# Second block of a two-block transformer kernel: plain float32 matmuls in place of three split products, a weight ring of eight slots, convolution taps and attention heads laid further ahead

## The chip, the cores and the metric

The kernel runs on one core of one Trainium2 chip. The metric is the device time of one launch in microseconds (us). The core has TensorE (PE in the profile, with PEld for its weight loads), VectorE (DVE), ScalarE (ACT), GpSimd (POOL), SyncE (SP, which only starts transfers here) and 16 DMA engines.

## The reference, cut to what matters

Two blocks run one after the other on 256 tokens of width 1024, in float32. The first (latent attention, Fourier and pooling branches, then a mixture over 16,384 experts whose rows are gathered) is not touched by the change. The second is this, with `T` = 256, `D` = 1024 and `D_FF` = 2816:

```python
for layer in range(2):
    f = swiglu_ffn(rms_norm(x, pre[layer, 0]), w_gate_up[layer, 0], w_down[layer, 0])
    x = x + 0.5 * rms_norm(f, post[layer, 0])
    h = rms_norm(x, mix_norm_pre[layer])
    if layer < 1:      # w_in 1024 -> 2048, GLU, causal convolution of 31 taps, LayerNorm, silu, w_out
        y = conformer_conv(h, ...)
    else:              # 8 heads of 128; with 256 tokens there is one block of keys, the own one
        q = h @ w_q;  k, v = split(rms_norm(x, g_kv) @ w_kv)
        y = causal_alibi_attention(q, k, v) @ w_o
    x = x + rms_norm(y, mix_norm_post[layer])
    f = swiglu_ffn(rms_norm(x, pre[layer, 1]), w_gate_up[layer, 1], w_down[layer, 1])
    x = x + 0.5 * rms_norm(f, post[layer, 1])
```

`swiglu_ffn(h)` is `(silu(gate) * up) @ w_down` with `gate, up = split(h @ w_gate_up)`.

## The kernel before, in words

Each engine has a program of its own, written out in one order of stages (`ORDER` for the first block, `ORDER2` for the second). The second block's stages are, for each of the six parts `f0`, `cv`, `f1`, `f2`, `at`, `f3`: `pre` (the norm, on DVE and ACT), `hT2` (16 transposes on PE), the part's inner stages, and `post` (norm and residual). Inner stages are `gu` and `dn` for a feed-forward part, `cin`, `taps`, `ln`, `cout` for the convolution, `qkv`, `moba`, `ao` for the attention.

Weights come in chunks of 1 MB (128 partitions x 2048 float32), 160 in all: 22 for each `gu`, 11 for each `dn`, 8 for `cin`, 12 for `qkv`, 4 for `cout` and 4 for `ao`. SP loads them into a ring of four slots (`SLOTS2`), three in `wring` and one in `rows`. In `gu`, `cin` and the k and q thirds of `qkv` (104 chunks) a chunk is used by `two_tiles`: 16 products, each with 128x128 weights stationary and 256 tokens moving. In `dn`, `cout`, `ao` and the v third of `qkv` (56 chunks) a chunk is used in 8 products, with the activations stationary and 512 weight columns moving.

Each product is made of three (`product`, lines 866 to 868). Both operands are split into an upper part of type float32r and a lower one (value minus upper part), and PE adds upper x upper, lower x upper and upper x lower. ACT writes the upper part of a chunk (`upper_of`, line 1288), DVE then the lower part (`lower_of`, line 1718); the transposed activations are split likewise (ACT line 1297, DVE line 1731), and so are the hidden values of a feed-forward part (DVE lines 1749 and 1751), the normed convolution output (1873, 1874) and each head's output (1396, 1895). `AHEAD` = 2 is how many chunks are split ahead of their use. The `gu` stages are hardware loops of five turns with four chunks each.

The products of the first block that are not gathers (for instance `gpre`, line 753, with the same shapes as `two_tiles`), the taps on PE (line 971) and the heads' scores and weighted sums (lines 1020 and 1036) are plain float32 matmuls.

In `cin` DVE and ACT make the gated values of 8 channel tiles; in `taps` DVE convolves four of them (31 steps each, line 1842) while PE convolves the other four by 124 matmuls with diagonal matrices, which ACT writes (line 1350) into a ring `diag` of 16. In `moba`, for head `hh`, PE makes the scores (1020), DVE adds the bias and takes the maximum (`biased`: 1887, 1890), ACT the exponential (1389), DVE reciprocal and scaling (1904, 1906), PE the transposes (1031) and the weighted sum (1036). Scores and `biased` run one head ahead.

SP's queue is in order. Ahead of the first chunk of the second block stand two loads of norm gains that wait for the first block's last residual (`x2` at 2).

## Time and profile before

| | |
|---|---|
| device time, median of 3 runs | 4663.01 us (4657.65 to 4663.29) |
| span of the profiled execution, first to last instruction | 4655.2 us |
| of it the second block (from 3461 us on) | 1194.2 us |
| PE busy over the span | 3150.5 us |
| PE busy in the second block | 1035.77 us |
| DVE and ACT busy in the second block | 694.50 and 464.94 us |

Of the profiled execution the span is what is known; it lies 7.8 us under the median of the three timed runs, and 2.5 us under the fastest. Changes are worked out on the span and carried over to the median. A busy PE is not a PE at its peak: a matmul's record holds its latency too, so consecutive records overlap, and what a product costs in a stream is read from the distance between starts.

### The profile page before, as it was taken

The page shows a single profiled execution, that of the slowest core. Times are in us where ns is not written, and L with a number is a line of the kernel's source. Part 1 is how long each engine was busy: PE and PEld are TensorE (multiplying, and loading weights), DVE is VectorE, ACT ScalarE, POOL GpSimd, SP SyncE. Part 2 cuts the span into 40 slices and gives each one's busy share as a digit, 9 for nine tenths or more (in the row PEclk, how much of TensorE's full clock was granted, in tenths as well). Part 3 has the DMA queues.
Part 4 walks back from the last instruction along what each step waited for, and adds up shares of the span by engine and source line. Part 5 has one row for each costly group of instructions (what it writes and reads, how often), then busy time and mean ns, then how long its engine had stood idle before and what let it go on. Part 6 is the DMA issues. An engine that isn't in the chain of part 4 may idle for free.

```text
span 4655.2 us, 42615 instructions
## 1 busy us (share of the span) xinstructions
PE 3150.5 (68%) x12636; PEld 1972.1 (42%) x12636; DVE 2902.3 (62%) x5798; ACT 961.8 (21%) x1932; POOL 1806.1 (39%) x1732
## 2 busy tenths in 40 slices
PE   6998346588755455555878633434449878898789
PEld 2476112254431111222535511111119768797688
DVE  2213996656689676666644788776666566565365
ACT  1211012111111001111122111111123353333333
POOL 0000566656566555666630277777740000000000
PEclk8999668799877777777889866677669989999799
DMA  4343779889988888889962588899975514544244
GB/s 187 137 151 134 234 264 343 299 339 358 333 321 298 313 322 333 306 322 345 382 246 87 172 305 304 315 337 343 345 289 173 176 42 158 188 166 172 82 167 154
DMA packets 273567, 1157.10 MB, mean 249 GB/s; under 512 B 30848, under 2 KB 31616, under 8 KB 234496
## 3 DMA queue, kind: packets, MB, share of 16 engines
q0 software_dynamic: 221184, 805.40, 47.9%
q1 hardware_dynamic: 52224, 349.75, 20.9%
q8 instruction: 78, 1.28, 0.1%
q14 instruction: 81, 0.66, 0.0%
HBM read 1153.99 MB, written 1.05 MB: 248 GB/s over the span
## 4 chain that ended last, share of the span: by engine, by line
PE 40%; DVE 24%; DMA 17%; issue 9%; POOL 8%; ACT 2%; POOLq 0%; DVEq 0%; SPq 0%; ACTq 0%
DMA rows<-in_peer_up,iup 10%; POOL rows L2052 8%; PE ps L866 7%; PE ps L867 6%; PE ps L868 6%; DVE accv L1633 6%; DMA rows<-in_peer_down,idown 6%; DVE rows L1616 5%; PE ps L827 4%; PE ps L753 3%; PE ps L595 3%; PE ps L798 2%; PE ps L554 2%; PE ps L776 1%; PE ps L971 1%
## 5 line engine op out<-in xcount | busy, mean ns | idle before, releaser
L827 PE MATMUL ps<-rows,diag 128*128 128x512 f32 x1536 | 1022.1, 791 | 1225.5 <-DMA rows<-in_peer_up,iup 1183.0
L827 PEld LDWEIGHTS ps<-rows,diag 128*128 128x128 f32 x1536 | 316.3, 238 | 1913.9 <-DMA rows<-in_peer_up,iup 1386.8
L2052 POOL DMA_INDIRECT rows<-in_peer_down,idown x768 | 879.8, 1146 | 543.5 <-DVE accv L1633 209.8
L2052 POOL DMA_INDIRECT rows<-in_peer_up,iup x768 | 853.8, 1112 | 390.0 <-issue 198.7
L1633 DVE SCALAR_TENSOR_TENSOR accv<-rows,act,accv 128x512 f32<-128x512 f32 x768 | 577.2, 752 | 341.8 <-DMA rows<-in_peer_up,iup 305.3
L1241 ACT ACTIVATE diag<-ident,act 128x128 f32<-128x128 f32 x768 | 277.3, 396 | 2146.0 <-PE ps L827 1666.8
L1616 DVE CUSTOM_DVE_ANT_0 rows<-rows,h_in 128x1024 f32<-128x1024 f32 x512 | 614.8, 1225 | 118.1 <-DMA rows<-in_peer_down,idown 105.6
L866 PE MATMUL ps<-hT_hi,w_hi 128*128 128x256 f32 x1600 | 452.7, 283 | 16.7 <-DVE hT_lo L1731 16.7
L867 PE MATMUL ps<-hT_hi,w_lo 128*128 128x256 f32 x1600 | 452.9, 283 | 0.0
L868 PE MATMUL ps<-hT_lo,w_hi 128*128 128x256 f32 x1600 | 450.7, 282 | 0.0
L1616 DVE CUSTOM_DVE_ANT_0 rows<-rows,h_ctx 128x1024 f32<-128x1024 f32 x256 | 311.0, 1225 | 118.4 <-DMA rows<-in_peer_down,idown 114.1
L1718 DVE TENSOR_TENSOR w_lo<-wring,w_hi 128x2048 fp32r<-128x2048 f32 x120 | 275.0, 2292 | 145.4 <-ACT w_hi L1288 143.6
L866 PEld LDWEIGHTS ps<-hT_hi,w_hi 128*128 128x128 f32 x1600 | 306.3, 191 | 18.3 <-issue 18.3
L868 PEld LDWEIGHTS ps<-hT_lo,w_hi 128*128 128x128 f32 x1600 | 304.0, 190 | 0.0
L867 PEld LDWEIGHTS ps<-hT_hi,w_lo 128*128 128x128 f32 x1600 | 303.9, 190 | 0.0
L2057 POOL COPY idown<-idx 128x8 uint32 (+1 forms) x96 | 27.2, 283 | 713.0 <-DVE gates L1602 712.6
L1288 ACT ACTIVATE w_hi<-wring 128x2048 fp32r<-128x2048 f32 x120 | 229.4, 1913 | 132.8 <-DMA wring<-in_wdn 83.5
L753 PE MATMUL ps<-hT,wring 128*128 128x256 f32 x1152 | 251.8, 379 | 0.0
L753 PEld LDWEIGHTS ps<-hT,wring 128*128 128x128 f32 x1152 | 218.8, 190 | 37.2 <-issue 7.4
L554 PE MATMUL ps<-wring,cvec 128*2 128x512 f32 x384 | 171.5, 622 | 31.9 <-DMA wring<-in_wmod 31.9
L798 PE MATMUL ps<-hT,wring 128*128 128x256 f32 x768 | 168.9, 379 | 2.0 <-ACT hT L1069 2.0
L798 PEld LDWEIGHTS ps<-hT,wring 128*128 128x128 f32 x768 | 144.8, 190 | 22.9 <-issue 4.0
(272 smaller groups left out, 3752.0 us busy)
## 6 DMA issues: line engine op xcount, KB each, us to landing
wring<-in_wgu SPq DMA_DIRECT2D x66, 1024.0 KB, 4.8
wring<-in_wmod SPq DMA_DIRECT2D x48, 1024.0 KB, 7.6
wring<-in_wG SPq DMA_DIRECT2D x36, 1024.0 KB, 8.0
wring<-in_wdn SPq DMA_DIRECT2D x33, 1024.0 KB, 4.8
wring<-in_wpq SPq DMA_DIRECT2D x24, 1024.0 KB, 5.0
rows<-in_wgu SPq DMA_DIRECT2D x22, 1024.0 KB, 4.8
wring<-in_wO SPq DMA_DIRECT2D x12, 1024.0 KB, 5.1
wring<-in_wout SPq DMA_DIRECT2D x12, 1024.0 KB, 4.9
```

Of the source, the lines that this page charges most:

```text
L554: last = pe.matmul(b[qd:qd + 2, :], cvec[:, 4 * half + k, :], w[:, k * 512:(k + 1) * 512], start=(half + k == 0), stop=(half == 1 and k == ...
L753: last = pe.matmul(b[:, dt * TOK:(dt + 1) * TOK], w[:, k * 256 + dt * P:k * 256 + (dt + 1) * P], hT[:, k, :], start=(k == 0), stop=(k == K ...
L798: last = pe.matmul(b[:, hp * TOK:(hp + 1) * TOK], w[:, k * 256 + hp * P:k * 256 + (hp + 1) * P], hT[:, k, :], start=(k == 0), stop=(k == K ...
L827: pe.matmul(ps[:, UPB, :], diag[:, j % DIAGS, :], rows[:, j, UPV:D], start=(first and j == 0), stop=(last and j == GROUP - 1), skip_group_ ...
L866: pe.matmul(out_, lh[l_at], rh[r_at], start=start, stop=False)
L867: pe.matmul(out_, ll[l_at], rh[r_at], start=False, stop=False)
L868: return pe.matmul(out_, lh[l_at], rl[r_at], start=False, stop=stop)
L1241: act.activation(diag[:, j % DIAGS, :], ident[:, :], ACT.Copy, scale=act8[:, j:j + 1]).then_inc(diag_ready, 1)
L1616: dve.tensor_tensor_reduce(out=rows[:, j, :], in0=rows[:, j, :], in1=h[s][:, t, :], scale=1.0, scalar=0.0, op0=ALU.mult, op1=ALU.add, accu ...
L1633: dve.scalar_tensor_tensor(accv[:, :], rows[:, j, 0:UPV], act8[:, j:j + 1], accv[:, :], ALU.mult, ALU.add).then_inc(upv_done, 1)
L1718: dve.tensor_tensor(W2_LO[c % SLOTS2], w, W2_HI[c % SLOTS2].bitcast(f32), ALU.subtract).then_inc(lo_ready, 1)
L2052: pool.indirect_dma_start(out=rows[:, j, :], out_offset=None, in_=table, in_offset=bass.IndirectOffsetOnAxis(ap=offs[:, j:j + 1], axis=0)) ...
```

## The change

The first block's computation is unchanged. In the second block:

- every weight product is one plain float32 matmul; the splits of chunks and activations, and the buffers for the parts, are gone. The `gu` loops are written out.
- the ring has eight slots (three in `wring`, one in `keysT`, four in `rows`). SP loads a chunk as soon as its slot is free, the first four without waiting for the first block's last residual; gains have places and semaphores of their own and are loaded one part ahead.
- the transposed activations are copied from PSUM half by ACT and half by DVE.
- `taps` is merged into `cin`: after each channel tile from the second on, DVE makes 6 of its 124 tap steps (two tiles at a time in turn), and ACT writes 6 diagonals into a ring of 48.
- in `moba` scores and `biased` run two heads ahead, the weighted sum of head `hh - 1` comes after the transposes of head `hh`, and buffers are four heads deep (`p2`) and two deep (`pT2`).

```diff
-SLOTS2 = 4
-AHEAD = 2
+SLOTS2 = 8
+DIAGS2 = 48
...
-            def product(out_, lhs, l_at, rhs, r_at, start, stop):
-                (lh, ll), (rh, rl) = lhs, rhs
-                pe.matmul(out_, lh[l_at], rh[r_at], start=start, stop=False)
-                pe.matmul(out_, ll[l_at], rh[r_at], start=False, stop=False)
-                return pe.matmul(out_, lh[l_at], rl[r_at], start=False, stop=stop)
...
                 for j in range(2):
                     for k in range(KT):
-                        last = product(b[:, j * TOK:(j + 1) * TOK], w, np.s_[:, k * 256 + j * P:k * 256 + (j + 1) * P], act_, np.s_[:, k, :],
-                                       start=(k == 0), stop=(k == KT - 1))
+                        last = pe.matmul(b[:, j * TOK:(j + 1) * TOK], w[:, k * 256 + j * P:k * 256 + (j + 1) * P], act_[:, k, :],
+                                         start=(k == 0), stop=(k == KT - 1))
...
                 for hh in range(H2):
-                    if hh + 1 < H2:
-                        scores(hh + 1)
+                    if hh + 2 < H2:
+                        scores(hh + 2)
...
-            def upper_of(c, landed):
-                act.wait_ge(chunk2_in[c % SLOTS2], landed)
-                act.activation(W2_HI[c % SLOTS2], W2[c % SLOTS2], ACT.Copy).then_inc(hi_ready, 1)
...
-                dve.tensor_tensor(W2_LO[c % SLOTS2], w, W2_HI[c % SLOTS2].bitcast(f32), ALU.subtract).then_inc(lo_ready, 1)
...
+                elif c == SLOTS:
+                    sp.wait_ge(mm_done, mm_at["sc", "x1", 7])
                 else:
-                    sp.wait_ge(x2, 2)
+                    sp.wait_ge(down_done, P * len(GATHERS))
...
-                v(dve.scalar_tensor_tensor(uth, uth, 1.0, usq, ALU.add, ALU.mult))
-                v(dve.tensor_copy(conv_2[0], uth))
-                dve.tensor_tensor(conv_2[1], uth, conv_2[0].bitcast(f32), ALU.subtract).then_inc(ln_s, 1)
+                dve.scalar_tensor_tensor(uth, uth, 1.0, usq, ALU.add, ALU.mult).then_inc(ln_s, 1)
```

The first place is PE's program at the start of `f0`: the transposes (`h_in`), then the first products of `gu`. Before, with buffer numbers kept (`w_hi_49` and `w_lo_53` are the parts of the first chunk):

```order
345 L881 MATMUL ps<-ident,h_in 128x128 x16
346 L901 UNCONDITIONAL_BRANCH
347 L901 ISA
348 L906 REGISTER_ALU
349 L866 MATMUL ps<-hT_hi,w_hi_49 128x256
350 L867 MATMUL ps<-hT_hi,w_lo_53 128x256
351 L868 MATMUL ps<-hT_lo,w_hi_49 128x256
```

The changed kernel at the same place, with the slots of the ring by their memory:

```order
345 L858 MATMUL ps<-ident,h_in 128x128 x16
346 L870 MATMUL ps<-hT,wring 128x256 x48
347 L870 MATMUL ps<-hT,keysT 128x256 x16
348 L870 MATMUL ps<-hT,rows 128x256 x64
349 L870 MATMUL ps<-hT,wring 128x256 x48
```

A chunk was 16 triples of matmuls and is 16 matmuls. For scale, `gpre` of the first block stands in the order before as `53 L753 MATMUL ps<-hT,wring 128x256 x48`, for three chunks.

The second place is SP's queue at the end of the first block, with the semaphores that each transfer waits for. Before:

```order
79 L1939 DMA wring<-in_wpq 128x2048 [waits mm_done] x6
80 L1945 DMA gain<-in_final_g 128x1024 [waits gain_used]
81 L2002 DMA gain<-in_ffn_pre 128x1024 [waits x2]
82 L2002 DMA mb<-in_ffn_post 128x1024 [waits x2]
83 L1993 DMA wring<-in_wgu 128x2048 [waits mm_done] x3
84 L1993 DMA rows<-in_wgu 128x2048 [waits x2]
```

And after the change:

```order
80 L1832 DMA gain<-in_final_g 128x1024 [waits gain_used]
81 L1913 DMA h_ctx<-in_ffn_pre 128x1024 [waits mm_done]
82 L1879 DMA wring<-in_wgu 128x2048 [waits mm_done] x3
83 L1879 DMA keysT<-in_wgu 128x2048 [waits mm_done]
84 L1879 DMA rows<-in_wgu 128x2048 [waits upp_done,upv_done,down_done] x4
```

Nothing ahead of the first four chunks waits for `x2` any more; the next four wait for the last gathered rows to be used.

The third place is the heads: PE's and DVE's programs around one head. PE before, from the transposes of head 0 on (`p2_ready` is DVE's scaling, a head's two tiles apart):

```order
4234 L1031 MATMUL ps<-ident,shared 128x128 [waits p2_ready,bank_free2]
4235 L1031 MATMUL ps<-ident,shared 128x128
4236 L1031 MATMUL ps<-ident,shared 128x128 [waits p2_ready]
4237 L1031 MATMUL ps<-ident,shared 128x128
4238 L1036 MATMUL ps<-shared,kvmem 128x256 [waits bank_free3,bank_free2]
4239 L1036 MATMUL ps<-shared,kvmem 128x256
4240 L1020 MATMUL ps<-kvmem 128x256 [waits bank_free0]
4241 L1020 MATMUL ps<-kvmem 128x256
```

PE in the changed kernel, from the transposes of head 1 on; line 982 is here the weighted sum of head 0, line 975 the scores of head 4:

```order
1847 L994 MATMUL ps<-ident,shared 128x128 [waits p2_ready,bank_free1]
1848 L994 MATMUL ps<-ident,shared 128x128
1849 L994 MATMUL ps<-ident,shared 128x128 [waits p2_ready]
1850 L994 MATMUL ps<-ident,shared 128x128
1851 L982 MATMUL ps<-shared,kvmem 128x256 [waits bank_free2,bank_free0]
1852 L982 MATMUL ps<-shared,kvmem 128x256
1853 L975 MATMUL ps<-kvmem 128x256 [waits bank_free4]
1854 L975 MATMUL ps<-kvmem 128x256
```

DVE in the changed kernel: bias and maximum of head 3 (they wait for `mm_done`, its scores), reciprocal and scaling of head 1, then bias of head 4:

```order
4374 L1772 SCALAR_TENSOR_TENSOR shared<-x_ctx,ps 128x256 [waits mm_done]
4375 L1772 SCALAR_TENSOR_TENSOR shared<-x_ctx,ps 128x256
4376 L1777 TENSOR_REDUCE nmax<-shared 128x1 [waits dve_step] x2
4377 L1791 RECIPROCAL rinv<-rsum 128x1 [waits e2_ready] x2
4378 L1796 TENSOR_SCALAR shared<-shared,rinv 128x256 [waits dve_step] x2
4379 L1772 SCALAR_TENSOR_TENSOR shared<-x_ctx,ps 128x256 [waits mm_done]
```

The order on PE is as before, transposes, weighted sum, scores; only the head that each belongs to has moved.

## Rows read from the trace of the kernel before

**Rows 1.** The profile page: its slices, and the costliest groups of the second block.
```profile
span 4655.2 us, 42615 instructions
...
PE   6998346588755455555878633434449878898789
...
L866 PE MATMUL ps<-hT_hi,w_hi 128*128 128x256 f32 x1600 | 452.7, 283 | 16.7 <-DVE hT_lo L1731 16.7
```

**Rows 2.** Windows: us, busy time (instructions) of each engine, granted clock, DMA share, GB/s.
```profile
3461.00:4655.20 1194.20, 1035.77 (x6824) 949.86 (x6824) 694.50 (x999) 464.94 (x560) 0.00 (x0) 0.92 0.43 148
...
3874.00:4000.20 126.20, 126.17 (x1057) 126.17 (x1058) 82.11 (x106) 46.89 (x43) 0.00 (x0) 0.99 0.52 175
...
4352.60:4414.80 62.20, 36.22 (x96) 23.41 (x96) 22.30 (x72) 18.92 (x50) 0.00 (x0) 0.63 0.05 17
```

**Rows 3.** Timeline of PE, split products: start us, us, what; `gu`, then `dn` of f3.
```profile
4500.00 0.28 PE L866 MATMUL ps<-hT_hi,w_hi 128*128 128x256 f32 x1
...
4501.76 0.28 PE L866 MATMUL ps<-hT_hi,w_hi 128*128 128x256 f32 x1
...
4583.03 0.39 PE L866 MATMUL ps<-w_hi,hid_hi 128*128 128x512 f32 x1
...
4643.52 0.40 PE L868 MATMUL ps<-w_lo,hid_hi 128*128 128x512 f32 x1
```

**Rows 4.** Timeline of PE, plain float32 products, and the row after each.
```profile
283.31 20.88 PE L753 MATMUL ps<-hT,wring 128*128 128x256 f32 x96
304.04 1.24 PE L776 MATMUL ps<-shared,wring 128*128 128x256 f32 x5
...
385.64 14.00 PE L595 MATMUL ps<-wring,shared 128*128 128x512 f32 x32
399.57 0.71 PE L540 MATMUL ps<-mrows,sel 2*128 2x512 f32 x4
...
3741.76 53.80 PE L971 MATMUL ps<-shared,diag 128*128 128x256 f32 x248 [0.94 <-ACT diag L1350]
```

**Rows 5.** Groups by line in the second block: the work of the splits, and DVE's taps.
```profile
L1718 DVE TENSOR_TENSOR w_lo<-wring,w_hi 128x2048 fp32r<-128x2048 f32 x120 | 275.0, 2292 | 145.4 <-ACT w_hi L1288 143.6
L1842 DVE SCALAR_TENSOR_TENSOR shared<-shared,mrows 128x256 f32<-128x256 f32 x120 | 47.6, 475 | 0.0
```

**Rows 6.** Waits of SP's queue; windows where x1's experts are ranked, and of its gathers.
```profile
SPq L2002 <- DVE x_in L1683: 873.6, 1, 873.6
...
2550.00:2600.00 50.00, 42.46 (x207) 37.79 (x208) 20.30 (x72) 6.84 (x12) 0.00 (x0) 0.90 0.38 132
...
3100.00:3300.00 200.00, 87.77 (x136) 25.74 (x136) 135.79 (x236) 24.77 (x75) 148.17 (x148) 0.71 0.95 345
```

**Rows 7.** Timeline of all engines at the start of f0 and of cv.
```profile
3477.14 3.68 PE L881 MATMUL ps<-ident,h_in 128*128 128x128 f32 x16 [16.20 <-DVE h_in L1700]
...
3490.19 0.58 PE L866 MATMUL ps<-hT_hi,w_hi 128*128 128x256 f32 x1 [9.38 <-DVE hT_lo L1731]
...
3695.35 0.35 PE L866 MATMUL ps<-hT_hi,w_hi 128*128 128x256 f32 x1 [1.72 <-DVE hT_lo L1731]
```

**Rows 8.** Timeline around the end of the LayerNorm.
```profile
3826.18 1.23 DVE L1873 CAST conv_hi<-shared 128x2048 fp32r<-128x2048 f32 x1
3827.44 2.29 DVE L1874 TENSOR_TENSOR conv_lo<-shared,conv_hi 128x2048 fp32r<-128x2048 f32 x1
```

**Rows 9.** Timeline of PE over one head, and its end.
```profile
4367.28 1.09 PE L1031 MATMUL ps<-ident,shared 128*128 128x128 f32 x4 [2.41 <-DVE shared L1906]
4369.05 2.07 PE L1036 MATMUL ps<-shared,kvmem 128*128 128x256 f32 x4 [0.69 <-ACT shared L1069]
4370.92 1.91 PE L1020 MATMUL ps<-kvmem 128*128 128x256 f32 x4
4375.24 0.81 PE L1031 MATMUL ps<-ident,shared 128*128 128x128 f32 x4 [2.41 <-DVE shared L1906]
...
4414.86 0.77 PE L866 MATMUL ps<-w_hi,attT_hi 128*128 128x512 f32 x1 [1.34 <-DVE attT_lo L1895]
```

More of the change, by code:

```diff
@@ L163, in block_stages @@
 def block_stages(tag):
-    inner = {"f": [("gu", tag), ("dn", tag)], "c": [("cin",), ("taps",), ("ln",), ("cout",)], "a": [("qkv",), ("moba",), ("ao",)]}[tag[0]]
+    inner = {"f": [("gu", tag), ("dn", tag)], "c": [("cin",), ("ln",), ("cout",)], "a": [("qkv",), ("moba",), ("ao",)]}[tag[0]]
     return [("pre", tag), ("hT2", tag)] + inner + [("post", tag)]
@@ L959, in cin @@
                     w = chunk2()
-                    ended(two_tiles(job2(("cin", c)), w, hT_2), ("cin", c))
+                    ended(two_tiles(job2(("cin", c)), w, hT), ("cin", c))
                     chunk2_end()
-            def taps():
                 for n, c in enumerate(range(TAPS_DVE, 8)):
@@ L1021, in scores, with weighted @@
                     ended(last, ("s2", hh))
+                def weighted(hh):
+                    at_evac(pe, ("pT2", hh))
+                    b = job2(("pv2", hh))
+                    for k in range(2):
+                        last = pe.matmul(b[:, 0:TOK], v2[:, k, hh * DH:(hh + 1) * DH], pT2[:, hh % 2, k, :], start=(k == 0), stop=(k == 1))
+                    ended(last, ("pv2", hh))
                 scores(0)
+                scores(1)
                 for hh in range(H2):
-                    if hh + 1 < H2:
-                        scores(hh + 1)
+                    if hh + 2 < H2:
+                        scores(hh + 2)
                     b = job2(("pT2", hh))
@@ L1335, in cin, with weights @@
                 act.wait_ge(conv_h, 1)
+                def weights(n0, n1):
+                    for k in range(n0, n1):
+                        n, j = divmod(k, TAPS)
+                        c = TAPS_DVE + n
+                        if k >= DIAGS2:
+                            act.wait_ge(mm_done, mm_at["tap", TAPS_DVE + (k - DIAGS2) // TAPS, (k - DIAGS2) % TAPS])
+                        w = 16 + j * 8 + c
+                        act.activation(diag2[:, k % DIAGS2, :], ident[:, :], ACT.Copy, scale=vec2[:, w:w + 1]).then_inc(tap_ready, 1)
                 for c in range(8):
-                    upper()
+                    weights(6 * c, 6 * c + 6)
                     b = at_mm(act, ("cin", c))
@@ L1761, in gu @@
-                split_no[0] += TURN * TURNS
-                for j in range(FT - TURN * TURNS):
-                    lower()
-                    key = ("gu", tag, j)
-                    kt = TURN * TURNS + j
-                    dst = tile(job_bank[key], j, kt, done + kt)
-                    at_evac(dve, key)
-                    parts(dst, j, done + kt)
-            def dn(tag):
-                lower(FT // 2)
-            def cout():
-                lower(4)
-            def ao():
-                lower(4)
@@ L1779, in qkv @@
-            def qkv():
-                lower(12)
+                for c in range(FT):
+                    key = ("gu", tag, c)
+                    b = at_mm(dve, key)
+                    dve.wait_ge(gate_th, done + c + 1)
+                    dve.scalar_tensor_tensor(ft2[:, c % 4, :], fth[:, c % 4, :], 1.0, b[:, 0:TOK], ALU.add, ALU.mult).then_inc(gu_step, 1)
+                    dve.wait_ge(gu_step, done + c + 1)
+                    dve.tensor_tensor(hid[:, c, :], ft2[:, c % 4, :], b[:, TOK:2 * TOK], ALU.mult).then_inc(hid_ready, 1)
+                    dve.wait_ge(hid_ready, done + c + 1)
+                    dve.sem_inc(bank_free[job_bank[key]], 1)
@@ L1852, in ln @@
+                while todo:
+                    tap(*todo.pop(0))
             def ln():
@@ new lines, in _ @@
+                    firsts[c] = args[0]
+                c += {"gu": FT, "dn": FT // 2, "cin": 8, "cout": 4, "qkv": 12, "ao": 4}.get(name, 0)
+            assert c == len(plan_2)
+            for c in range(len(plan_2)):
+                chunk2()
+                if c - SLOTS2 in firsts:
+                    beside_block(firsts[c - SLOTS2])
+            sp.wait_ge(x2, X2_AT["f3"])
+            sp.dma_start(out.rearrange("(t p) d -> p t d", p=P), x[0][:, :, :]).then_inc(out_done, 16)
+            sp.wait_ge(out_done, 16)
```

455 lines of the change are left out of this document (179 added, 276 removed).

## The prediction

> **What bounds the kernel now.** I first looked for the second block in the page's slices: a slice is 4655.2/40 = 116 us, and the last ten of PE's row read 9878898789 [rows 1], so PE is busy there nearly all the time. The windows give that a size: from 3461 us on PE is busy in 1035.77 of 1194.20 us, DVE in 694.50 and ACT in 464.94 [rows 2]. One `gu` stage alone (3874.0 to 4000.2) has PE busy throughout at a granted clock of 0.99, with DVE at 82.11 us of 126.20 and the DMA engines at 0.52 [rows 2]; line 866 sat idle for 16.7 us in all before its 1600 large products [rows 1]. So in the stages that read weights the matmul stream sets the time, and the splits on ACT and DVE, though large (DVE's lower parts take 2.292 us per chunk, 160 of them 367 us [rows 5]), lie beside it. PE waits elsewhere: between the parts, in the LayerNorm, and in `moba`, where it is busy in 36.22 of 62.20 us [rows 2].
>
> The price of a product must be read from the distance between starts. Split, 256 columns: from 4500.00 to 4501.76 us are 15 matmuls, 0.1175 us each, so 0.353 us for the three of a product [rows 3]. Split, 512 columns: 4583.03 to 4643.52 us are 263 distances, 0.230 us each, 0.690 us a product [rows 3].
>
> Plain float32, 256 columns, same shapes: the row of line 753 has 96 records from 283.31 to 304.04 us [rows 4]. It is easy to read this wrongly. 20.73/96 = 0.216 us looks like 39% less than three split matmuls. But the program issues 48 matmuls there for three chunks, not 96: each plain matmul leaves **two records**. A second place agrees: 124 tap instructions leave 248 records in 53.80 us [rows 4]. So a plain product of 256 columns takes 2 x 0.216 = 0.432 us, and one of 512 columns 2 x 13.93/32 = 0.871 us (line 595, 385.64 to 399.57 us [rows 4]). The three split matmuls leave one record each (16 x 100 chunks = 1600 of line 866 [rows 1]).
>
> The page FP8 and Floating Point Precision of the Trainium skill (TensorE Precision Notes) says that true FP32 is four passes through the array. The doubled records, each as long as two passes of 256 columns at 2.4 GHz, agree. By passes alone plain would cost 4/3 of three split products, more than the rows show (0.432/0.353 = 1.22), because in the rows a split matmul costs more than a bare pass.
>
> **The change part by part, on PE.** `two_tiles` chunks: 16 products, 16 x 0.432 = 6.91 us now against 16 x 0.353 = 5.65 us: +1.26 us, on 104 chunks +131 us. The other 56 chunks have 8 products of 512 columns: 8 x 0.871 = 6.97 against 8 x 0.690 = 5.52: +1.45 us, in all +81 us. **Sum +212 us**, all on the path, since PE has no slack in these stages. For one `gu` that is 22 x 1.26 = 28 us on 126, for one `dn` 11 x 1.45 = 16 us on 61.
>
> **What comes off.** Splitting is hidden except where a stage starts.
> - Start of f0: PE ends its transposes at 3480.82 and starts products at 3490.19, 9.38 us later [rows 7], because the first chunks come only once SP is past the gains that wait for the residual, and are then split. SP stood in that wait for 873.6 us [rows 6]. Now four chunks are there long before; only a copy of the last transposes remains, as at cv without its split: 1.72 us [rows 7] less one of two copies in series, so about 0.8. **-8.6 us**.
> - The other five parts: 1.72 us falls to some 0.8: **-4.5 us**.
> - LayerNorm: the copy and the subtraction that split its output go, 1.23 and 2.29 us [rows 8]: **-3.5 us**.
> - Taps: PE's 53.80 us stay [rows 4], since the matmuls are the same plain ones. DVE's taps lie beside (120 x 0.475 us [rows 5]); a third of them are made earlier, under `cin`, which has 6.91 us per tile for 2.9 us of taps. That frees DVE and nothing else. What goes is PE's 0.94 us wait for the first diagonal [rows 4]: **-0.9 us**.
> - Heads. One head now takes 4375.24 - 4367.28 = 7.96 us: transposes 1.09, wait 0.69 for the copy of them, weighted sum 2.07, scores 1.91, wait 2.41 for DVE (overlaps make up the rest) [rows 9]. "Further ahead" moves heads, not the ring. PE makes the scores of head `hh + 2` only after the transposes of `hh - 1`, and DVE biases `hh + 2` ahead of scaling `hh`; so PE still waits some 2.5 us in every head for a DVE step that waits for the scores just made. What goes is the 0.69 us wait: the weighted sum is now of the head before, whose copy is done. That makes 7.1 us for each of five heads; the last two, with no scores before them, take about 3 us each instead of 7.5; three biases instead of two stand ahead of the first transposes, each under the 2.41 us of a whole DVE step, and cost some 2 us more. At the end only ACT's copy is left of the 1.34 us [rows 9]. I sum the heads to 54 us from 62: **-7.8 us**. The bound above is no gain at all, the bound below a row's clock twice as fast, under the rivals.
>
> What costs nothing: transfers. A chunk per 6.9 us is 152 GB/s, less than the 175 now [rows 2]; the ring of eight hides it even without that. The four chunks loaded early are issued when x1's last first-block chunks are used, while experts are ranked; the DMA share there is 0.38 [rows 6]. If they fell into the gathers instead they would cost 4.2 MB at the 345 GB/s at which gathers run [rows 6], 12 us. The next four wait for the last gather, about 20 us before f0's fifth chunk is wanted. ACT and DVE lose work and gain none that is waited for: the copies of the transposes are shared between them, and the gated products of `gu` stay what they are, under a longer matmul stream.
>
> Sum: 212 - 8.6 - 4.5 - 3.5 - 0.9 - 7.8 = **+187 us**. On the span that is 4655.2 + 187 = 4842 us; on the median, 7.8 us above that span, **4850 us**, 4.0% slower.
>
> **The rivals.**
> 1. *Warm heads.* In `moba` the granted clock is 0.63 [rows 2]; the scores at 1.91 us for four records are at the 1.2 GHz level. With less waiting it may stay at 2.4 GHz, which halves PE's 5 us of a head: a head takes 5.2 us, the heads lose another 14 us. 4836 us. Against it: PE would still be idle a third of the time in stretches of 2.5 us, as in the rows that are slow now. 13%.
> 2. *The early chunks, or SP's new order, hold up the gathers or a gain.* +12 us as above, 4862 us. Against it: the low DMA share at that point. 7%.
> 3. *Passes only.* If weights that change with every matmul cost a plain pass as much as a split one, a plain product takes 4/3 of 0.353 = 0.471 us; 4/3 of all split work (104 x 5.65 + 56 x 5.52 = 897 us) is +299, less 25 that come off, so 4937 us. Against it: the taps and line 753 change weights with every matmul too [rows 4]. 1%. (It is what the four passes of the page named above would make of the split rows.)
> 4. *The other side: plain products are cheaper than I read.* The mechanism is that a plain matmul costs one record, 0.216 us per 256 columns, and the second record is of something that overlaps. Then weight work falls by 897 - 554 = 343 us and the time would be near 4290. It decides the sign from 0.363 us a product down, where the extra cost no longer exceeds the 25 us that come off. For it: counted record by record the rows do read 0.216 against 3 x 0.118. Against it: 96 records fill 20.73 us of wall time for three chunks, and nothing in that stretch but these 48 matmuls keeps PE. 2%.
>
> **How the numbers follow.** The forecast has 75%, and 2% are for what I do not see, half of it within 0.2% of before and half faster. Its own range: the +212 carries perhaps 4 us of reading error, the 25 us that come off may be 12 to 35, the runs lie 6 us apart: 4835 to 4868. Warm heads and held gathers widen it by little, to **4828 to 4870**. A measurement of this kernel can tell about 0.2%, 9 us, from no change. Faster by more than that: rival 4 and the 1%, together 3%; within it 1%; slower 96%.
>
> **What would show it.** PE rows of `gu` with 32 records per chunk and 0.216 us between starts, a `gu` stage of about 154 us and a `dn` of about 77; products of f0 some 1 us after its transposes; PE's waits for DVE of about 2.5 us in most heads; 53.6 us for the taps; PE's waits for chunks absent. Wrong would be: one record per plain matmul in the second block, a `gu` under 130 us, PE waiting for DMA inside a stage, or a first block that ends later than 3461 us.

## The result and the profile after

The changed kernel takes 4823.92 us (median of 4 runs, 4818.87 to 4835.82) against 4660.33 us (4653.66 to 4663.29, 4 runs) of the kernel before on the same chip: a ratio of 1.0358, interval 1.0333 to 1.0383. It is slower by 164 us, where +187 was forecast; the time is 26 us under the forecast and 4 us under the lower end of the range.

**The page of the changed kernel**: its span, PE's row of slices, and the group of the largest products (the name is that of the slot in `rows`).

```profile
span 4824.0 us, 36981 instructions
...
PE   6998355687845555557786343444498979899799
...
L870 PE MATMUL ps<-hT,rows 128*128 128x256 f32 x1472 | 322.5, 381 | 3.3 <-DVE hT L1653 3.3
```

As in [rows 1], PE is busy nearly throughout the last slices, and nothing but DVE's copy of the transposes delayed a product of this group, by 3.3 us in all. A chunk leaves 32 records: 46 of the 104 chunks are in this group, 46 x 32 = 1472.

**The start of f0 and one `gu` and `dn`**, timeline of PE (start us, us, what, idle time before):

```profile
3484.54 3.67 PE L858 MATMUL ps<-ident,h_in 128*128 128x128 f32 x16 [16.17 <-DVE h_in L1643]
3489.30 6.07 PE L870 MATMUL ps<-hT,wring 128*128 128x256 f32 x27 [1.09 <-DVE hT L1653]
```
```profile
3922.68 2.61 PE L870 MATMUL ps<-hT,rows 128*128 128x256 f32 x11 [1.09 <-DVE hT L1653]
```
```profile
4074.70 7.03 PE L889 MATMUL ps<-keysT,shared 128*128 128x512 f32 x16
4081.56 27.63 PE L889 MATMUL ps<-rows,shared 128*128 128x512 f32 x64
4109.03 1.45 PE L889 MATMUL ps<-wring,shared 128*128 128x512 f32 x3
```

Products of f0 start 1.09 us after the transposes, where 9.38 us stood [rows 7]. The `gu` of f1 lasts from 3922.68 to 4074.70, 152.02 us for 22 chunks or 0.432 us a product, against about 126 before [rows 2]. In `dn` 80 records fill 4074.70 to 4109.03, 0.429 us each, so 0.858 us a product against 0.690 [rows 3].

**End of `cin`, taps, and the wait of the LayerNorm**, timeline of PE (line 906 is `cout`):

```profile
3784.06 7.07 PE L870 MATMUL ps<-hT,wring 128*128 128x256 f32 x32
3790.97 53.72 PE L926 MATMUL ps<-shared,kvmem 128*128 128x256 f32 x248
3844.53 3.62 PE L940 MATMUL ps<-shared,x_ctx 128*128 128x256 f32 x16
...
3874.65 15.52 PE L906 MATMUL ps<-wring,shared 128*128 128x512 f32 x32 [16.08 <-DVE shared L1759]
```

The 248 tap records stay as in [rows 4], and the 0.94 us ahead of them is gone. PE's idle time between the second sum of the LayerNorm and `cout` is 16.08 us where the kernel before has 19.67: the cast and the subtraction of [rows 8] are gone.

**One head**, all engines, from 4520 us on (`shared` holds the scores, `L1796` is the scaling):

```profile
4520.61 1.09 PE L994 MATMUL ps<-ident,shared 128*128 128x128 f32 x4 [2.05 <-DVE shared L1796]
...
4521.49 1.92 PE L982 MATMUL ps<-shared,kvmem 128*128 128x256 f32 x4
...
4523.20 1.91 PE L975 MATMUL ps<-kvmem 128*128 128x256 f32 x4
...
4525.15 0.75 DVE L1772 SCALAR_TENSOR_TENSOR shared<-x_ctx,ps 128x256 f32<-128x256 f32 x2 [4.42 <-PE ps L975]
4525.82 0.74 DVE L1777 TENSOR_REDUCE nmax<-shared 128x1 f32<-128x256 f32 x2
...
4526.48 0.21 DVE L1791 RECIPROCAL rinv<-rsum 128x1 f32<-128x1 f32 x2
4526.67 0.62 DVE L1796 TENSOR_SCALAR shared<-shared,rinv 128x256 f32<-128x256 f32 x2
...
4527.16 1.09 PE L994 MATMUL ps<-ident,shared 128*128 128x128 f32 x4 [2.05 <-DVE shared L1796]
```

This is the same stretch of the loop as in [rows 9], here from the transposes of head 3 to those of head 4. The 0.69 us wait for ACT is gone. The ring, in which each engine waits once a head for the other, is still there: scores on PE, then bias, maximum, reciprocal and scaling on DVE, then transposes on PE; PE stands for 2.05 us (2.41 before), DVE for 4.42. The exponentials of the head to be scaled are long done, but DVE takes the scaling up behind the bias of a later head, whose scores PE has only just made.

**The transposes of heads 0, 1, 2 and 5**, timeline of PE:

```profile
4504.78 0.63 PE L994 MATMUL ps<-ident,shared 128*128 128x128 f32 x4 [3.03 <-DVE shared L1796]
...
4508.68 1.09 PE L994 MATMUL ps<-ident,shared 128*128 128x128 f32 x4 [2.05 <-DVE shared L1796]
...
4515.01 0.63 PE L994 MATMUL ps<-ident,shared 128*128 128x128 f32 x4 [2.05 <-DVE shared L1796]
...
4533.71 1.09 PE L994 MATMUL ps<-ident,shared 128*128 128x128 f32 x4 [2.05 <-DVE shared L1796]
```

The first turn is 3.90 us: no weighted sum stands in it, and PE ran part of it at full clock. The next two are 6.33 and 5.60, the last two 6.55. Where the four transposes take 0.63 us PE runs at 2.4 GHz (granted 1.00), where they take 1.09 at 1.2 GHz (granted 0.50).

**Windows** (columns as in [rows 2]) of the second block, of the heads, and of the first 4 us of products in f0, cv, f1, f2 and f3:

```profile
3484.50:4824.00 1339.50, 1225.90 (x4712) 902.80 (x4712) 242.33 (x608) 145.15 (x376) 0.00 (x0) 0.95 0.36 126
...
4497.60:4541.00 43.40, 27.93 (x96) 20.66 (x97) 16.84 (x64) 17.17 (x49) 0.00 (x0) 0.69 0.07 25
```
```profile
3489.30:3493.30 4.00, 4.00 (x19) 3.54 (x20) 0.00 (x0) 0.00 (x0) 0.00 (x0) 1.00 0.00 0
3733.50:3737.50 4.00, 3.95 (x9) 3.20 (x10) 0.36 (x3) 1.86 (x6) 0.00 (x0) 0.50 0.00 0
3922.70:3926.70 4.00, 4.00 (x19) 3.54 (x20) 0.00 (x0) 0.00 (x0) 0.00 (x0) 1.00 0.00 0
4166.90:4170.90 4.00, 3.99 (x10) 3.19 (x11) 0.00 (x0) 0.00 (x0) 0.00 (x0) 0.50 0.00 0
4585.00:4589.00 4.00, 3.97 (x19) 3.54 (x20) 0.00 (x0) 0.00 (x0) 0.00 (x0) 1.00 0.02 4
```

The heads take 43.4 us where they took 62.2 [rows 2]. Of these 18.8 us, 8.3 are PE's own time (27.93 for 36.22 us, at a granted clock of 0.69 for 0.63) and 10.5 are idle time. Runs 4 and 5, which leave the heads as they are, repeat them (43.5 and 43.4 us, clock 0.69), and run 6 has 44.5.

**Where the 161 us lie.** The first block is the same code in both, and its end moves from run to run: the transposes of f0 start at 3477.14 us before, 3484.54 after, and between 3472.20 and 3497.61 us over the 13 profiled runs here. That the first block ended 7.4 us later, which the prediction names among its signs of being wrong, lies within this scatter. So I compare from those transposes to the end of the span: 1178.1 us before, 1339.5 after, +161.4. Below, "length" is always this one. Each length is of one profiled execution. The intervals of the ratios are some 12 us to either side, so a difference between two runs that is smaller than that rests on the stages of these executions and not on the timed runs. By stages:

| term | predicted us | measured us |
|---|---|---|
| products of 160 chunks | +212 | +198.0 (`gu` +105.2, `dn` +59.2, the other 28 chunks +33.6) |
| start of f0 | -8.6 | -8.3 |
| the other five starts | -4.5 | -4.0 |
| LayerNorm | -3.5 | -3.6, and its second sum -0.7 |
| taps | -0.9 | -1.0 |
| heads | -7.8 | -18.8 |
| norms, residuals, transposes | 0 | -0.4 |
| sum | +187 | +161.2 of the 161.4 |

### The profile page after: what moved, and what is told of

It reads as the page before. It is cut to its first block, busy times and chain, and to the rows that moved or that the text cites. A ratio compares the mean times of both kernels' runs of the same rounds, so it can differ in the third digit from the quotient of the medians.

```text
span 4824.0 us, 36981 instructions
## 1 busy us (share of the span) xinstructions
PE 3333.1 (69%) x10524; PEld 1924.5 (40%) x10524; DVE 2459.8 (51%) x5438; ACT 647.1 (13%) x1758; POOL 1810.2 (38%) x1732
## 3 DMA queue, kind: packets, MB, share of 16 engines
q1 hardware_dynamic: 52224, 349.75, 19.8%
## 4 chain that ended last, share of the span: by engine, by line
PE 43%; DVE 22%; DMA 15%; issue 9%; POOL 9%; ACT 1%; POOLq 0%; DVEq 0%; SPq 0%; ACTq 0%
PE ps L870 15%; DMA rows<-in_peer_up,iup 9%; POOL rows L1938 8%; PE ps L889 6%; DVE accv L1570 6%; DVE rows L1553 5%; DMA rows<-in_peer_down,idown 5%; PE ps L812 4%; PE ps L738 3%; PE ps L783 2%; PE ps L580 2%; PE ps L906 2%; PE ps L539 2%; PE ps L761 1%; PE ps L926 1%
## 5 line engine op out<-in xcount | busy, mean ns | idle before, releaser
L812 PEld LDWEIGHTS ps<-rows,diag 128*128 128x128 f32 x1536 | 315.4, 237 | 1924.8 <-DMA rows<-in_peer_up,iup 1382.1
L870 PE MATMUL ps<-hT,rows 128*128 128x256 f32 x1472 | 322.5, 381 | 3.3 <-DVE hT L1653 3.3
L1661 DVE SCALAR_TENSOR_TENSOR shared<-shared,ps 128x256 f32<-128x256 f32 x88 | 37.0, 421 | 540.9 <-ACT shared L1244 540.9
L870 PEld LDWEIGHTS ps<-hT,rows 128*128 128x128 f32 x1472 | 281.0, 191 | 43.3 <-issue 4.9
L870 PE MATMUL ps<-hT,wring 128*128 128x256 f32 x1344 | 294.8, 381 | 2.2 <-DVE hT L1653 2.2
L870 PEld LDWEIGHTS ps<-hT,wring 128*128 128x128 f32 x1344 | 256.7, 191 | 38.1 <-issue 2.9
L738 PE MATMUL ps<-hT,wring 128*128 128x256 f32 x1152 | 253.6, 381 | 0.0
L738 PEld LDWEIGHTS ps<-hT,wring 128*128 128x128 f32 x1152 | 220.1, 191 | 37.7 <-issue 7.4
L889 PE MATMUL ps<-rows,shared 128*128 128x512 f32 x416 | 179.8, 592 | 0.0
L1689 DVE TENSOR_TENSOR h_ctx<-ps,mb 128x512 f32<-128x512 f32 x20 | 13.7, 691 | 323.5 <-ACT h_in L1033 323.5
L783 PE MATMUL ps<-hT,wring 128*128 128x256 f32 x768 | 171.3, 383 | 2.0 <-ACT hT L1030 2.0
L783 PEld LDWEIGHTS ps<-hT,wring 128*128 128x128 f32 x768 | 146.4, 192 | 23.7 <-issue 4.1
L889 PEld LDWEIGHTS ps<-rows,shared 128*128 128x128 f32 x416 | 79.0, 190 | 98.2 <-issue 98.1
```

The costliest lines, as they stand in the source:

```text
L738: last = pe.matmul(b[:, dt * TOK:(dt + 1) * TOK], w[:, k * 256 + dt * P:k * 256 + (dt + 1) * P], hT[:, k, :], start=(k == 0), stop=(k == K ...
L783: last = pe.matmul(b[:, hp * TOK:(hp + 1) * TOK], w[:, k * 256 + hp * P:k * 256 + (hp + 1) * P], hT[:, k, :], start=(k == 0), stop=(k == K ...
L812: pe.matmul(ps[:, UPB, :], diag[:, j % DIAGS, :], rows[:, j, UPV:D], start=(first and j == 0), stop=(last and j == GROUP - 1), skip_group_ ...
L870: last = pe.matmul(b[:, j * TOK:(j + 1) * TOK], w[:, k * 256 + j * P:k * 256 + (j + 1) * P], act_[:, k, :], start=(k == 0), stop=(k == KT ...
L889: last = pe.matmul(bs[n], hid[:, 2 * c + k, t * P:(t + 1) * P], w[:, k * D + half * 512:k * D + (half + 1) * 512], start=(c + k == 0), sto ...
```

## The experiments

The theory that they test: (a) products alone cost some 200 us; (b) the heads are a ring of PE and DVE whose length is set by the order on DVE, not by how many heads lie between; (c) what the clock grants in the heads and at the start of a stage moves the rest by a few us. The rivals are named with each run.

**1. Plain products alone**, in the kernel before (the splits are still made, the lower parts are left out of the products):

```diff
-                pe.matmul(out_, lh[l_at], rh[r_at], start=start, stop=False)
-                pe.matmul(out_, ll[l_at], rh[r_at], start=False, stop=False)
-                return pe.matmul(out_, lh[l_at], rl[r_at], start=False, stop=stop)
+                return pe.matmul(out_, lh[l_at].bitcast(f32), rh[r_at].bitcast(f32), start=start, stop=stop)
```

> The kernel before with one edit: each product is one plain float32 matmul of the two upper parts instead of three split matmuls; ACT and DVE still write both parts, so ring, order, heads and taps are those of before. The lower parts are left out of the result. Theory (the price of the products is what the change costs, and the rest gives back): the time is 4660 plus the difference of the products. By the trace of after, a gu stage took 152 us against 126, a dn 75.5 against 60.9; summed over all weight stages 198 us, so 4858 us, above the changed kernel's 4824. With the prices of the prediction it would be 4660 + 212 = 4872. Rival (the products cost less by themselves, and something else of the change, such as the written-out loops or the ring, makes the stages long): below 4840.

4867.46 us (5 runs, 4861.38 to 4885.42), ratio 1.0456 [1.0430, 1.0481]; length 1382.1, +204.0 us. The heads stay at 61.9 us. The price of the products stands by itself, about 8 us under the 212 forecast, and all else in the change takes off 42.6 us (1382.1 to 1339.5), not 25. Of these 42.6, some 6 lie in the product stages themselves: here they are 204.6 us longer than before and not 198.0, because the `gu` of f0 and f1, `cout` and `ao` ran more of their start at half clock (`ao` 30.44 us for 27.71), and only f2's `gu` less. At full clock a `gu` is 152.0 and a `dn` 75.7 us here too, with hardware loops and a ring of four; so neither the written-out loops nor the ring of eight changed the length of these stages.

**2 and 3. The two halves of "further ahead" in `moba`**, each undone in the changed kernel. First the weighted sum goes back behind the transposes of its own head (PE here, ACT likewise):

```diff
-                    if hh:
-                        weighted(hh - 1)
-                weighted(H2 - 1)
+                    weighted(hh)
```

> The changed kernel with the weighted sum of a head right after its own transposes again, scores and bias still two heads ahead. The heads took 62.3 us before and 43.4 after. Theory 1 (what shortens the heads is that the weighted sum no longer waits for the copy of its own head's transposes): a head goes back to about 7.5 us from 6.55, the heads to about 52 us, the time is some 8 us over the changed kernel's 4824. Theory 2 (it is the two heads of distance): the heads stay near 43 us, no change beyond 2 us.

Then scores, exponentials and bias run one head ahead (PE here, ACT and DVE likewise):

```diff
-                scores(1)
                 for hh in range(H2):
-                    if hh + 2 < H2:
-                        scores(hh + 2)
+                    if hh + 1 < H2:
+                        scores(hh + 1)
```

> The changed kernel with scores, bias and exponential one head ahead instead of two, and the weighted sum still one head behind. Theory 1 (PE and DVE form a ring in each head whatever the distance, and only the lag helps): a head stays at 6.5 us, one more of them has scores ahead of it, so the heads take 45 to 48 us instead of 43.4 and the time is within 4 us of the changed kernel's. Theory 2 (distance is what helps): the heads go back to 55 us or more, the time is 12 us or more over the changed kernel's.

| kernel | median us | ratio, interval | length | heads us | PE busy, idle in them | clock in them |
|---|---|---|---|---|---|---|
| after | 4823.92 | 1.0358 [1.0333, 1.0383] | 1339.5 | 43.4 | 27.9, 15.5 | 0.69 |
| own weighted sum | 4838.27 | 1.0374 [1.0348, 1.0401] | 1346.6 | 50.6 | 29.6, 21.0 | 0.80 |
| one head ahead | 4815.62 | 1.0338 [1.0317, 1.0359] | 1339.2 | 43.9 | 26.8, 17.1 | 0.77 |

The intervals overlap, so the reading is from the stages. The distance of two heads is worth little beyond one: 0.5 us (43.9 for 43.4), made of 1.6 us less waiting and 1.1 us more of PE's own time at the lower clock. The weighted sum's lag is worth 7.2 us, of which 5.5 are PE's waits for the copy, eight times 0.69. PE's timeline of the kernel without the lag, at full clock for the transposes:

```profile
4531.47 0.63 PE L994 MATMUL ps<-ident,shared 128*128 128x128 f32 x4 [2.05 <-DVE shared L1792]
4532.79 2.08 PE L982 MATMUL ps<-shared,kvmem 128*128 128x256 f32 x4 [0.69 <-ACT shared L1028]
...
4538.31 0.63 PE L994 MATMUL ps<-ident,shared 128*128 128x128 f32 x4 [2.05 <-DVE shared L1792]
```

The 0.69 us is back, and the 2.05 us did not leave: both waits are there, and a head is 6.84 us. The wait for DVE ahead of the transposes is 2.05 us in all three, as (b) has it (3.03 or 2.58 us for the first head). It was 2.41 us before, so the 0.36 us comes neither from the lag nor from the distance. What is left of the edit is DVE's new form: two biases, then two maxima, and likewise two reciprocals, then two scalings, instead of one after the other with a wait behind each. DVE's rows agree: from the first bias of a head to the next scaling were 1.87 us before (4372.87 to 4374.74) and are 1.52 now. No run undid that form alone.

**4. The first four chunks held back** until the first block's residual:

```diff
                     sp.wait_ge(mm_done, chunk_done[last])
+                    if c == 0:
+                        sp.wait_ge(x2, 2)
```

> The changed kernel with its first chunk of the second block, and so all behind it in the queue, held back until the first block's last residual, as before. In the profiled executions the gathers of x1 took 836.2 us before (2624.1 to 3460.3) and 843.7 us after (2624.1 to 3467.8). Theory 1 (the gathers vary from run to run; the early chunks neither help nor harm, since a chunk that is asked for at the residual lands before f0's transposes end): within 3 us of the changed kernel. Rival 1 (the early chunks slow the gathers by the 7.5 us seen): 5 to 8 us faster than the changed kernel. Rival 2 (early loading was worth most of the 8 us that f0's start lost): 4 to 8 us slower, with PE waiting for the first chunk.

4821.16 us (5 runs, 4805.60 to 4825.57), ratio 1.0345 [1.0322, 1.0368]; length 1341.6, and the wait ahead of f0's products is 1.09 us as before the edit. Early chunks show neither a cost in the gathers nor a gain. The first block ends no later with them: the transposes of f0 start at 3480.0 us in the mean of the seven profiled kernels that load four early, at 3480.2 in the four that hold them all back. SP issues the first chunk at 3472.97 us here, the first product starts at 3482.59, and in these 9.6 us the chunk lands while the norm and the transposes are still made. The 2.1 us of the length are a `gu` of f0 that began at half clock (154.3 us for 152.0). So what removed f0's 9.38 us was not the early load but that nothing has to be split behind it. The kernel before fits this: its first chunk was issued as late (3473.06) and had landed when ACT began to split it at 3480.64, as the transposes ended (3480.81); then ACT and DVE split two chunks ahead of the transposed activations.

**5. Five channel tiles on DVE**, three on PE:

```diff
-TAPS_DVE = 4
+TAPS_DVE = 5
...
-                    for _ in range(6 if c else 0):
+                    for _ in range(10 if c else 0):
```

> The changed kernel with five channel tiles convolved on DVE instead of four, 10 tap steps after each tile of cin instead of 6, and 93 instead of 124 tap matmuls on PE. Theory (laying DVE's taps under cin gained nothing in the change because PE's own 124 taps of 0.432 us set the end; it frees DVE for work that can be moved over): PE's taps fall from 53.6 to 40.2 us, DVE has 85 steps of about 0.47 us left, 40 us, so the LayerNorm starts 13 us earlier and the time is 12 to 13 us under the changed kernel's. Rival (DVE's steps are slower beside PE and ACT, or ten of them do not fit under a tile of cin): the gain is under 6 us, and PE waits for DVE at the mean.

4806.48 us (5 runs, 4791.61 to 4813.60), ratio 1.0302 [1.0280, 1.0323]; length 1326.8, -12.7 us. PE's taps, and the row behind them:

```profile
3792.49 40.33 PE L926 MATMUL ps<-shared,kvmem 128*128 128x256 f32 x186
3832.65 3.62 PE L940 MATMUL ps<-shared,x_ctx 128*128 128x256 f32 x16
```

31 taps less on PE are 62 records and 13.4 us; DVE had the room. The taps laid under `cin` brought nothing in the change because PE's share of them, which set the stage, was left as it was.

**6. A second copy at each part's start**, so that PE waits longer there:

```diff
+                        if t:
+                            v(dve.tensor_copy(dst[:, 4:8, t * P:(t + 1) * P], b))
                         release(dve.tensor_copy(dst[:, 4:8, t * P:(t + 1) * P], b), key)
```

> The changed kernel with DVE's copy of the second token tile's transposes made twice, so that PE stands idle some 1.8 us instead of 1.09 us between the transposes and the first product of each part, as long as before. Before, four of six parts began their products at half clock (granted 0.50 to 0.63 in the first 4 us), after the change two of five looked at. Theory (the shorter idle time lets more parts begin at full clock): most parts begin at half clock again, each such start costs about 2 us beside the 0.7 us of the copy, in all 8 to 10 us over the changed kernel. Rival (which parts begin at half clock is chance): only the copies show, 4 us.

4829.10 us (5 runs, 4820.66 to 4838.51), ratio 1.0366 [1.0346, 1.0386]; length 1344.7, +5.2. Five waits are 1.82 us instead of 1.09 and `at` starts 0.2 us later, in all 3.9 us; the other 1.4 are clock (`gu` of f0 and f3 and the heads longer by 1.4, 1.7 and 1.1 us, `cin` and `gu` of f2 shorter by 2.1 and 0.7). Windows of the first 4 us of f1's and f2's products:

```profile
3913.90:3917.90 4.00, 4.00 (x19) 3.53 (x20) 0.00 (x0) 0.00 (x0) 0.00 (x0) 1.00 0.00 0
4158.90:4162.90 4.00, 4.00 (x12) 3.33 (x13) 0.00 (x0) 0.00 (x0) 0.00 (x0) 0.64 0.00 0
```

f1 (and cv, also 1.00) starts at full clock behind a wait of 1.8 us, cv and f2 of the changed kernel at half clock behind 1.09. f0 and f3 went the other way (0.65 and 0.58 here, 1.00 there). So the length of the last wait alone does not decide it.

**7 and 8. The new heads without plain products**, in the kernel before: first `moba` alone as after the change (PE here; ACT, DVE and the deeper buffers likewise, with the split of each head's output kept, two heads late), then also the first chunks of f0 loaded and split while its norm is made.

```diff
-                    if hh + 1 < H2:
-                        scores(hh + 1)
+                    if hh + 2 < H2:
+                        scores(hh + 2)
...
-                    at_evac(pe, ("pT2", hh))
-                    b = job2(("pv2", hh))
...
+                    if hh:
+                        weighted(hh - 1)
+                weighted(H2 - 1)
```

> The kernel before (split products, ring of four) with the heads of the changed kernel: scores two ahead, the weighted sum one behind, DVE's lower part of a head's output two heads behind. Theory (the heads' gain does not hang on the plain products): the heads fall from 62 to about 45 us, the time from 4660 to about 4644 us. Rival (DVE's extra step per head stands in the ring, or the lower parts wait): under 8 us.

> As the run with split products and new heads, and in addition the first three chunks of the second block are loaded ahead of the gains without waiting for the residual, ACT splits two of them while DVE norms, DVE one. Theory (f0's 9.4 us of idle PE were the late chunks and their splitting): PE waits about 2.5 us there, another 6 us come off, about 4638 us. Rival (DVE's part in the middle of the norm costs what it saves): within 2 us of the run without it.

New heads: 4635.25 us (6 runs, 4625.82 to 4642.59), ratio 0.9939 [0.9921, 0.9957]; length 1152.9, -25.2: the heads take 39.5 us (62.3 before, clock 0.87), and `ao`, which now begins at full clock, 2.5 us less. Some of it is luck: the next run has the same heads and took 44.1 us for them at a clock of 0.73, with the same 16 us of idle time. With the first chunks too: 4630.27 us (6 runs, 4614.92 to 4642.54), ratio 0.9933 [0.9911, 0.9955]; length 1146.8. PE's start of f0 there:

```profile
3473.78 3.67 PE L881 MATMUL ps<-ident,h_in 128*128 128x128 f32 x16 [17.08 <-DVE h_in L1718]
3479.24 0.38 PE L866 MATMUL ps<-hT_hi,w_hi 128*128 128x256 f32 x1 [1.79 <-DVE hT_lo L1747]
```

9.38 us became 1.79, of which the first lower part gives 0.9 back in the norm ahead (17.08 for 16.2), outside the length. The length gains 6.1 us: 7.4 from the wait (9.17 in the run without it) and 3.2 from two `gu` that began at a higher clock, less the 4.7 of the colder heads. The two medians, 5.0 us apart, do not show it surely. The gains of the new heads and of an f0 without late splitting do not hang on the plain products.

**9. Scaling ahead of the next bias**, in the changed kernel (DVE here; ACT copies before its exponentials likewise):

```diff
                 for hh in range(H2):
-                    if hh + 2 < H2:
-                        biased(hh + 2)
                     at_ = []
...
                         dve.tensor_scalar(pp, pp, rinv[:, c:c + 1], None, ALU.mult).then_inc(p2_ready, 1)
+                    if hh + 2 < H2:
+                        biased(hh + 2)
```

> The changed kernel with DVE's order in the heads turned round: reciprocal and scaling of head hh come ahead of bias and maximum of head hh + 2, and ACT copies the transposes of hh ahead of the exponentials of hh + 2. Theory (in the changed kernel PE and DVE still wait for each other in every head, 2.05 us each time, because DVE biases a head whose scores PE has only just made before it scales the one PE is waiting for; two heads of distance are there but not used): PE's waits of 2.05 us go, a head takes about 3 us, the heads fall from 43.4 to about 27 us. Rival (DVE or ACT, with about 2.4 us a head each, or the clock, becomes the bound): 3.5 us or more a head, the heads stay over 33 us. The second block is compared by its own length, since the first block's varies by some 20 us from run to run.

4806.35 us (5 runs, 4794.73 to 4810.57), ratio 1.0318 [1.0299, 1.0336]; length 1320.7, -18.8. PE's timeline and the window of its heads:

```profile
4498.55 0.63 PE L994 MATMUL ps<-ident,shared 128*128 128x128 f32 x4
4499.02 1.03 PE L982 MATMUL ps<-shared,kvmem 128*128 128x256 f32 x4
4499.88 1.03 PE L975 MATMUL ps<-kvmem 128*128 128x256 f32 x4
4500.75 0.60 PE L994 MATMUL ps<-ident,shared 128*128 128x128 f32 x4
```
```profile
4486.20:4509.90 23.70, 18.47 (x98) 14.70 (x97) 16.79 (x64) 16.36 (x49) 0.00 (x0) 1.00 0.13 45
```

A head takes 2.2 us, without a wait on PE, at a clock of 1.00; with the waits it took 6.55. DVE is as full: from 4492.2 to 4505.0 us it is busy for 12.37 of 12.80 us, PE for 11.71. The wait was the order of steps, scaling behind the next bias on DVE; ACT's copy was moved ahead with it and was not tried apart. Scaling first with a distance of one head was not run either, so how much of this gain needs the distance of two is not shown.

**10. DVE's step made longer** by two idle maxima in each `biased`:

```diff
+                        if t == 0:
+                            for _ in range(2):
+                                v(dve.tensor_reduce(nmax[:, c:c + 1], p2[:, hh % 4, t, :], axis=AX.X, op=ALU.max, negate=True))
```

> The changed kernel with one of DVE's maxima in each head made three times, so that PE waits about 1 us longer in each head. In the heads the granted clock was 0.63 with PE idle 26.0 of 62.2 us (before), 0.69 to 0.87 with some 16 us idle of 40 to 44. Theory (longer idle stretches push the heads back to half clock, so that the cost is more than the added waits): beside 8 us of waits, PE's busy time in the heads rises from 27.9 to 34 us or more and the clock falls to 0.6 or below, heads 55 us or more. Rival (the clock there is chance): 50 to 52 us.

4830.17 us (4 runs, 4819.45 to 4839.32), ratio 1.0375 [1.0353, 1.0397]; length 1345.4, +5.9; heads 50.2 us. PE's timeline:

```profile
4499.91 1.09 PE L994 MATMUL ps<-ident,shared 128*128 128x128 f32 x4 [2.96 <-DVE shared L1799]
4500.79 1.92 PE L982 MATMUL ps<-shared,kvmem 128*128 128x256 f32 x4
4502.50 1.15 PE L975 MATMUL ps<-kvmem 128*128 128x256 f32 x4
4506.60 1.09 PE L994 MATMUL ps<-ident,shared 128*128 128x128 f32 x4 [2.96 <-DVE shared L1799]
```

Five waits grew from 2.05 to 2.96 us, 4.6 us in all, and the first, behind three biases, from 3.03 to 5.75; less 0.5 us of PE's own time these make the 6.8 us by which the heads grew. The 0.90 us that DVE has more between bias and scaling is paid one for one by PE. The clock did not fall for all of the head: the transposes ran at its lower level (1.09 us), the scores partly at the upper (1.15 us for 1.91). Against the theory of this run, longer waits alone did not make the heads colder.

**11. The best of both**: the kernel before with the new heads, the early first chunks and the scaling first (runs 8 and 9 together).

> The kernel with split products, the changed kernel's heads and the early first chunks, and in addition scaling ahead of the next bias in the heads. Theory: as in the changed kernel some 13 us come off the heads (39 to 26 us), DVE's lower part of each head's output (0.42 us) costing a little of it; the second block from its first transposes on falls from 1146.8 to about 1134 us, the time to about 4620 us, faster than both kernels. Rival (DVE, now with 2.8 us a head, holds PE up): under 6 us.

4607.41 us (6 runs, 4592.91 to 4626.52), ratio 0.9895 [0.9871, 0.9919]; length 1129.9, -48.2, without the 0.9 us in the norm ahead; its heads take 25.1 us at a clock of 1.00:

```profile
4344.20:4369.30 25.10, 18.84 (x97) 14.71 (x97) 19.51 (x72) 17.16 (x50) 0.00 (x0) 1.00 0.13 42
```

It is faster than both kernels, by 0.8 to 1.3% than the one before, and it keeps the split products.

## Why the prediction was right in kind and 26 us off

**Right.** Plain products bound the result: a plain matmul leaves two records, a product of 256 columns costs 0.432 us, and run 1 prices them alone at +204 us. *Passes only* (4937) and the rival of cheaper plain products (near 4290) are refuted by it. *Held gathers* finds no support in run 4 and its means, which would show 12 us. The starts, the LayerNorm and the taps came out within 0.5 us each, its second sum apart. That "further ahead moves heads, not the ring" holds by runs 2, 3, 9 and 10: PE waited for DVE in every turn but the last one or two until the order on DVE changed.

**Two terms of the sum were mis-sized and failed: the heads, -7.8 us for -18.8, and the products, +212 for +198.** Together they are 25 of the 26 us. In the heads the mechanism stood; the term was 11 us off, in three places of its sum, of which the first is part of the second. (1) "PE still waits some 2.5 us": it waits 2.05. (2) "7.1 us for each of five heads" makes 35.5; the six starts of transposes, from 4504.78 to 4533.71, lie 28.9 us apart. The first turn, 3.90, has no weighted sum in it, which I had not taken out; it and the next two ran partly at full clock (6.33 and 5.60 us for the 6.55 of the others). (3) Ends: 14.5 us for the 18.5 that I summed; the three first scores cost 0.5 us more than before and not 2. *Warm heads*, which I held apart as a rival at 4836, was no separate case: the clock alternated within one `moba`, and its mean was 0.69 to 0.87 over kernels with the same 2.05 us wait.

**The products are 14 us less than the +212.** A plain product of 512 columns is 0.858 us, not 0.871: the row of line 595 in [rows 4] ran up to a row of another kind, and 13.93/32 held that switch; on 448 products it is 5.8 us. The four split `gu` all began wholly or partly at half clock (0.50, 0.53, 0.62 and 0.63 in their first 4 us), of the plain ones only f2's. At full clock throughout, a split `gu` took 124.5 us (f0 in run 8) and a plain one 152.0: the split ones lost 7.1 us in all, the plain ones 2.2, so 5 us came off that a price "from the distance between starts" could not hold. `ao` gained 2.5 us in the same way, behind warmer heads (25.3 us before, 22.7 in run 7), and `cin` lost 2.1 (57.4 us, and 55.3 in run 6). Of the 3 us left, part is rounding in the split prices (a `dn` of 60.89 us is 0.692 us a product, not 0.690). The prediction's own rows held the sign: it puts a split `gu` at 126 us by the window, while 22 chunks of 5.65 are 124.3; and it forecasts a `gu` of 154 us where its price gives 22 x 6.91 = 152.0, which is what was measured.

The range put 4 us of error on the products and 10 us on what comes off; they came to 14 and 11.5 us, the same way. A part of both has one reason: half-clock stretches of the kernel before were in its time but not in my prices.

## What to carry to other kernels

Count the records that one instruction leaves before pricing it, and take a price from the middle of a long run of its kind, not up to the next row. Compare a stage's whole length with its price too; here the difference was the half-clock start. In a loop over heads it is worth little to run further ahead as long as an engine in the ring takes up new work before the step that its neighbour waits for: put the step that is waited for first (-18.8 us here, against 0.5 for the second head of distance alone). When an edit brings several things, price each apart: the rest of the change gained here about 43 us, 6 of them clock, that the plain products' 204 hid; and with the new heads and starts on split products, and the scaling first, the kernel is 1.1% faster than before.

## What was unexpected of the hardware

Stages that began behind the same wait began at different clocks. In the changed kernel f0, f1 and f3 had 1.00 in their first 4 us and cv and f2 0.50, all behind a wait of 1.09 us, and a `gu` that starts at half clock costs some 2 us (154.2 for 152.0 us). Mostly this went by place and not by run: in all seven profiled kernels with this wait (the changed one and runs 2, 3, 4, 5, 9 and 10; for f3 it was 1.26 us in three) f1 and f3 started at 1.00 and took 152.0 us, cv started at 0.50 to 0.58, and f2 at 0.50 and took 154.1 to 154.3. Only f0 varied, from 1.00 in four of them to 0.50, 0.52 and 0.54 in three. The page TensorE: Matmul & The Clock Gate of the Trainium skill (its Part 1) says that the point at which the clock rises varies from run to run. f0 agrees with that; the other four starts do not show it. What decides it in one place was not found; by run 6 it is not the length of the last wait alone.

In the heads PE never kept full clock where it waited 2.05 us for DVE in each head: the mean was 0.69 to 0.87 in eight kernels, and in the same loop the four transposes took 0.63 us in one turn and 1.09 in another. With waits of at most 0.9 us from the second head on (runs 9 and 11) it was 1.00, and PE ran transposes, weighted sums and scores in 0.63, 1.03 and 1.03 us. Of the 19.8 us that run 9 took off the heads, 9.5 are PE's own time (27.93 to 18.47 us busy) and the rest is waiting. No run shows why the clock in a turn came out one way or the other: two kernels with the same heads and the same idle time had 0.87 and 0.73 (runs 7 and 8).
